# An encoder layer on one core: small loads awaited at the first transposes, the last query latents turned six units later, buffers from `hidden` on shifted by 32 bytes

## What is computed

```python
x = x + 0.5 * swiglu_ffn(rms_norm(x, ffn1_norm_g[l]), ffn1_w_gate[l], ffn1_w_up[l], ffn1_w_down[l])
h = rms_norm(x, mix_norm_g[l])
u = h @ w_in[l]
u_conv, c_q_raw, c_kv_raw, k_rope_raw, gl_conv, gl_mla = jnp.split(u, IN_SPLITS, axis=-1)
y_conv = conformer_conv_branch(u_conv, ...)      # 31-tap depthwise convolution, layer norm, silu, matmul
y_mla = mla_branch(c_q_raw, c_kv_raw, k_rope_raw, ...)   # 16 heads, q from 768 latents, k and v from 512
merged = jax.nn.sigmoid(gl_conv) * y_conv + jax.nn.sigmoid(gl_mla) * y_mla
x = x + merged @ w_out[l]
x = x + 0.5 * swiglu_ffn(rms_norm(x, ffn2_norm_g[l]), ffn2_w_gate[l], ffn2_w_up[l], ffn2_w_down[l])
return rms_norm(x, final_norm_g)
```

## Time and profile before

| | |
|---|---|
| median of 3 runs | 2376.14 us (2375.38 to 2376.43) |
| the profiled execution | 2375.09 us |
| its span, first to last instruction | 2373.1 us |
| mean granted TensorE clock | 0.996 |
| TensorE busy | 2319.3 us (98%), 10718 matmuls and transposes |
| VectorE, ScalarE busy | 1322.5 us (56%), 1188.6 us (50%) |
| DMA | 432.65 MB, 182 GB/s over the span |

### The profile page before, as it was taken

One profiled execution on the slowest core, in us unless ns is written; L12 is line 12 of the kernel. 1 busy time (PEld: TensorE's weight loads), 2 busy tenths in 40 slices (PEclk: granted clock), 3 DMA queues, 4 the chain that ended last, 5 costly groups with the idle time before them and its releaser, 6 DMA issues.

```text
span 2373.1 us, 26781 instructions
## 1 busy us (share of the span) xinstructions
PE 2319.3 (98%) x10718; PEld 1926.1 (81%) x10718; DVE 1322.5 (56%) x1469; ACT 1188.6 (50%) x1619; POOL 0.2 (0%) x4
## 2 busy tenths in 40 slices
PE   5999999999999999989999999999999999999997
PEld 4888888888888888868889878888888888888886
DVE  4554544544544588978876455655544544544443
ACT  5444444444444577777767564445444444444433
POOL 0000000000000000000000000000000000000000
PEclk9999999999999999999999999999999999999999
DMA  6666666666655655546643456556656656656663
GB/s 229 192 189 187 192 189 188 193 187 185 186 184 182 194 188 186 181 147 203 192 146 116 132 164 184 186 179 203 194 186 189 192 187 189 193 186 186 187 188 131
DMA packets 120588, 432.65 MB, mean 182 GB/s; under 512 B 13584, under 2 KB 13840, under 8 KB 120208
## 3 DMA queue, kind: packets, MB, share of 16 engines
q1 hardware_dynamic: 120464, 430.93, 58.7%
HBM read 428.78 MB, written 2.10 MB: 182 GB/s over the span
## 4 chain that ended last, share of the span: by engine, by line
PE 96%; DVE 2%; issue 1%; ACT 1%; DMA 1%; SPq 0%; ACTq 0%; DVEq 0%
PE bank L663 31%; PE bank L662 31%; PE bank L661 31%; PE turned L672 2%; PE bank L799 1%; PE bank L773 1%; PE bank L774 1%; DMA pos_i<-in_pos_in 0%; DVE q_rope L1083 0%; DVE w_lo L900 0%; ACT w_hi L422 0%; DVE q_rope L1089 0%; PE turned L784 0%; DMA raw<-in_ffn_up 0%; PE turned L853 0%
## 5 line engine op out<-in xcount | busy, mean ns | idle before, releaser
L900 DVE TENSOR_TENSOR w_lo<-raw,w_hi 128x1024 fp32r<-128x1024 f32 (+2 forms) x814 | 987.1, 1215 | 995.0 <-ACT w_hi L422 994.6
L422 ACT ACTIVATE w_hi<-raw 128x1024 fp32r<-128x1024 f32 (+2 forms) x814 | 853.6, 1052 | 1039.1 <-PE bank L663 1035.8
L661 PE MATMUL bank<-w_hi,h 128*128 128x512 f32 (+1 forms) x2144 | 836.3, 390 | 28.0 <-DMA pos_i<-in_pos_in 26.4
L663 PE MATMUL bank<-w_hi,h 128*128 128x512 f32 (+1 forms) x2144 | 833.4, 389 | 0.0
L662 PE MATMUL bank<-w_lo,h 128*128 128x512 f32 (+1 forms) x2144 | 833.2, 389 | 0.0
L661 PEld LDWEIGHTS bank<-w_hi,h 128*128 128x128 f32 x2144 | 403.7, 188 | 110.8 <-DMA pos_i<-in_pos_in 26.4
L663 PEld LDWEIGHTS bank<-w_hi,h 128*128 128x128 f32 x2144 | 403.3, 188 | 82.7
L662 PEld LDWEIGHTS bank<-w_lo,h 128*128 128x128 f32 x2144 | 403.5, 188 | 81.6
L661 PE MATMUL bank<-w_hi,hidden 128*128 128x512 f32 x704 | 278.8, 396 | 0.0
L662 PE MATMUL bank<-w_lo,hidden 128*128 128x512 f32 x704 | 278.4, 395 | 0.0
L663 PE MATMUL bank<-w_hi,hidden 128*128 128x512 f32 x704 | 278.4, 395 | 0.0
(11 more groups left out here) (167 smaller groups left out, 1223.2 us busy)
## 6 DMA issues: line engine op xcount, KB each, us to landing
raw<-in_ffn_up SPq DMA_DIRECT2D x352, 512.0 KB, 4.0
raw<-in_ffn_down SPq DMA_DIRECT2D x176, 512.0 KB, 3.6
raw<-in_conv_in SPq DMA_DIRECT2D x64, 512.0 KB, 3.9
raw<-in_conv_gate SPq DMA_DIRECT2D x32, 512.0 KB, 4.0
raw<-in_mla_gate SPq DMA_DIRECT2D x32, 512.0 KB, 4.2
raw<-in_mla_out SPq DMA_DIRECT2D x32, 512.0 KB, 3.6
raw<-in_conv_out SPq DMA_DIRECT2D x32, 512.0 KB, 3.7
raw<-in_w_out SPq DMA_DIRECT2D x32, 512.0 KB, 3.6
```

The source lines that it names most:

```text
L422: act.activation(w_hi[:, j, 0:n], raw[:, j, 0:n], ACT.Copy).then_inc(hi_ready, 1)
L661: pe.matmul(dst, fixed_hi, moving_hi, start=first, stop=False)
L663: return pe.matmul(dst, fixed_lo, moving_hi, start=False, stop=last)
L900: dve.tensor_tensor(w_lo[:, j, 0:n], raw[:, j, 0:n], w_hi[:, j, 0:n], ALU.subtract).then_inc(lo_ready, 1)
```

## The change

Six edits. TensorE's wait for the four small loads moves from ahead of unit 0 to the first turn (after unit 17). `x` is loaded in four column pieces, after units 4, 5, 6 and 7, instead of whole after unit 3; its squares, root and factor move one step later (7 and 8, and 9). ScalarE runs a copy of two zeros ahead of its first wait, with which its function table is loaded. The third turn of `cq_raw` and the turn of `k_rot` move from after unit 356 to after unit 362, and the work that takes them follows on ScalarE and VectorE at step 366. The turns back of the layer norm begin one unit later. And `before_hidden`, 8 floats a partition, stands ahead of `hidden`, so that `hidden` and all that is allocated after it (`attn`, `merged`, `c_kv`, `c_q` and the rest) begin 32 bytes later, at multiples of 64. `k_rot`'s turn now waits for 7 steps of `key_step` instead of 5.

```diff
--- before.py
+++ after.py
...
-TURNS = {"up": (2, 1, 1), "resid": (2, 2, 2), "glu": (2, 1, 0), "kv": (2, 2, 2), "q1": (3, 2, 2),
+TURNS = {"up": (2, 1, 1), "resid": (2, 2, 2), "glu": (2, 1, 0), "kv": (2, 2, 2), "q1": (2, 2, 2),
          "qrope": (2, 1, 0), "merge": (2, 1, 1)}
 
 TURN_AFTER = {"kv": 4, "q1": 5}
+
+LATE_TURN_AFTER = 11
...
+        self.q_turn = self.more_turns(1, 2, 2)
         self.k_turn = self.more_turns(1, 2, 0)
...
+        sb("before_hidden", [P, 8])
...
         hidden = sb("hidden", [P, FT, 2, T], F32R, outs)
...
-        FORE, BACK = M0 + 6, M0 + 20
+        FORE, BACK = M0 + 6, M0 + 21
...
             for u in range(KT // DEEP):
                 sp.dma_start(xt[:, DEEP * u:DEEP * (u + 1), :], xt_in[:, DEEP * u:DEEP * (u + 1), :]).then_inc(xt_loaded[u], 16)
                 load(u)
-                if u == 3:
-                    sp.dma_start(x[:, :, :], x_in).then_inc(x_loaded, 16)
+                if u >= 4:
+                    cols = slice(WIDE * (u - 4), WIDE * (u - 3))
+                    sp.dma_start(x[:, :, cols], x_in[:, :, cols]).then_inc(x_loaded, 16)
...
+            act.wait_ge(table_input, 1)
+            act.activation(root[:, :], total[:, :], ACT.Copy).then_inc(table_loaded, 1)
             act.wait_ge(gains_loaded, 16)
...
+                if u - AHEAD == Q_END + LATE_TURN_AFTER:
+                    take_late_turns()
-                if u == 8:
+                if u == 9:
                     take_root("x0")
-                if u in (6, 7):
-                    act.wait_ge(x_loaded, 16)
-                    tt = u - 6
+                if u in (7, 8):
+                    act.wait_ge(x_loaded, 64)
+                    tt = u - 7
...
             def turn_group(n):
                 g = groups[n]
+                if n == 1:
+                    pe.wait_ge(small_loaded, 64)
...
+            def late_turns():
+                pe.wait_ge(scaled, 4)
+                turn(plan.q_turn, cq_raw, 4 * P)
+                n = plan.k_turn
+                pe.wait_ge(*turn_freed(n - 2))
+                pe.wait_ge(key_step, 7)
+                for tt in range(2):
+                    last = pe.transpose(turned_bank[n % 2][:, tt * P:(tt + 1) * P],
+                                        k_rot[:, tt, :, :].rearrange("p d c -> p (d c)"), identity[:, :])
+                last.then_inc(turned, 1)
...
-            pe.wait_ge(small_loaded, 64)
             u = 0
...
                 turn_after(u)
+                if u == Q_END + LATE_TURN_AFTER:
+                    late_turns()
...
+            def take_late_turns():
+                dve.wait_ge(turn_hi, turns[plan.q_turn].hi_before + 2)
+                for r in range(2):
+                    dve.scalar_tensor_tensor(out=c_q[:, 4 + r, 1, :], in0=turned_bank[plan.q_turn % 2][:, r * T:(r + 1) * T],
+                                             scalar=gain["q"][:, 4 + r, :], in1=c_q[:, 4 + r, 0, :], op0=ALU.mult,
+                                             op1=ALU.subtract).then_inc(turn_lo, 1)
...
+            dve.memset(total[:, :], 0.0).then_inc(table_input, 1)
             dve.wait_ge(gains_loaded, 16)
...
                 if u == 8:
                     variance("x0", 1, D)
+                if u == 9:
                     factor("x0", rstd)
```

More of the change, by code:

```diff
@@ L293, in encoder @@
         scaled = sem("scaled")
+        table_input = sem("table_input")
+        table_loaded = sem("table_loaded")
         xt_hi = sem("xt_hi")
@@ L493, in take_turns @@
                         act.activation(q_rope[:, k:k + 2, 0, :], pair, ACT.Copy).then_inc(turn_hi, 1)
[L494 to L500, removed]
+            def take_late_turns():
+                act.wait_ge(turned, plan.q_turn + 1)
+                for r in range(2):
+                    act.activation(c_q[:, 4 + r, 0, :], turned_bank[plan.q_turn % 2][:, r * T:(r + 1) * T], ACT.Copy,
+                                   scale=gain["q"][:, 4 + r, :]).then_inc(turn_hi, 1)
+                t = turned_bank[plan.k_turn % 2]
+                act.wait_ge(turned, plan.k_turn + 1)
+                act.wait_ge(cleared, 4)
+                for j in range(2):
+                    rows = slice(ROPE * j, ROPE * (j + 1))
+                    act.activation(k_rope[rows, j, :], t[rows, 0:T], ACT.Copy).then_inc(turn_hi, 1)
             def make_tap(n):
@@ L733, in wait_stationary @@
                 elif g.stage == "q_rope":
-                    t = turns[plan.stage("latents")[2].turn + 2]
+                    t = turns[plan.q_turn]
                     pe.wait_ge(turn_lo, t.lo_before + t.lo)
@@ L950, in finish @@
                     if g.stage == "ffn1_down" and g.i == 0:
-                        dve.wait_ge(x_loaded, 16)
+                        dve.wait_ge(x_loaded, 64)
                     for tt in range(2):
```

## The result

| | before | after |
|---|---|---|
| median | 2375.76 us (2374.68 to 2376.43, 4 runs) | 2339.9 us (2339.5 to 2340.69, 4 runs) |
| profiled execution | 2375.09 us | 2340.69 us |
| its span | 2373.1 us | 2338.9 us |
| mean granted TensorE clock | 0.996 | 0.998 |

The ratio is 0.9851, 95% interval 0.9839 to 0.9864. The kernel became 35.9 us faster, where 49 were forecast: the direction was right, and the time lies 13.3 us above the forecast and 5.9 above the top of its range.

The account below looks back on a forecast made before the run. TensorE's stream was taken as the bound (96% of the span). Start 18.3, turn 10.0, layer norm 1.5 and addresses 19.7 sum to 49.5 us: 2325.6 from the profiled execution, 2326.6 as median; range 2321 to 2334.

Parts of the forecast that it names:

- The address term: Streams with `hidden`, `attn`, `merged`, `c_q` stationary: starting at multiples of 64 bytes gives `h`'s pace, 19.7 us (0 to 22).
- the shift does nothing: Rival on the buffers' addresses: moving them 32 bytes gains nothing, time 2346 us; chance 0.11.
- The start: Before unit 0: with the small-load wait moved, first matmul at 8.1 instead of 26.45 us; gain 18.3, at least 17.6.
- The table of the units' spare: Units 4 to 11 at the start: each ready before TensorE wants it, spare 4.1 down to 0.5 us; priced 0.
- The turn: Query latents' turn near unit 357: moving late transposes removes the 8.5 us wait and half clock; gain 10.0 (7.5 to 10.5).
- the 0.5 us of new waits: After the query latents' turn: VectorE, losing its pause, causes new short TensorE waits of 0.5 us, bounds 0 and 3.
- The layer norm: Layer norm's turns back: starting one unit later covers the 1.5 us wait; gain 1.5 us, 0 if the wait moves along.
- The rivals on the start: Start runs dry: slower `x` pieces or ScalarE detours make TensorE wait 2 to 6 us, 2329 to 2333; chance 0.08.
- on VectorE: Rival in the gate stages: VectorE's backlog makes TensorE wait in pieces, 2329 to 2333 us; chance 0.06.
- on slower: Rival after unit 357: continued waits drop the clock; above 2376 us if over 20 units run at half clock; chance 0.02.

## Why the prediction was wrong, point by point

**The address term failed, and it makes the miss.** It was put at 19.7 us and is 3.8 to 4.1 by the pad alone, and 4.9 in the table of places (1.4 + 1.7, and 1.8 in q_rope and the heads). By medians it was 15.9 too much, and the other three parts together gave 2.3 more than forecast; 49.5 - 15.9 + 2.3 = 35.9. The step that failed is "What differs is the byte at which they begin: 0 or 32 past a multiple of 64". The first half is true, and the runs show that the byte was the cause. The second half picked one property out of several in which 128 and 160 differ, and the trace of before had no buffer at a third multiple of 64 to tell them apart. `h` was fast because `w_hi` and `w_lo` begin at the same 128. The shift took `hidden` from 32 ahead of them to 64 ahead, 233 ns and 233 ns: **hidden 14.1 -> 0**. It took `attn` and `merged` from 96 behind to 64 behind, 233 to 229: **5.1 -> 3.1**. And it touched the heads, for which nothing was counted: **0 -> some 1.5**; `c_q` in q_rope gave 0.3 of its 0.5.

**The rival "the shift does nothing"** came nearer: 2346 against 2339.9. It would have been a better forecast for a wrong reason, since the address does count. What I should have had as a case of its own is a shift that misses, or helps only some of the buffers. The text had the bound, lower end 0, and then left it outside the range, with a chance of 0.11.

What the Trainium skill says (SBUF - State Buffer, Operand start alignment), that a start need only be a multiple of the element's size, is right for what runs; it gives no time, and the runs above differ by 13 us through starts alone. The lines of 16 bytes (same page, Specifications) don't tell these starts apart either: all are multiples of 32.

**The start was right in its mechanism and somewhat high in size.** 18.3 was forecast, at least 17.6. The first matmul came at 8.35 instead of 8.1, 18.1 earlier than before, of which 17.2 were left from unit 20 on; undone alone it was 18.7. The table of the units' spare held: no matmul waits between 8.35 and 994.83, and of units 4 to 11 the least spare is unit 11's, 1.3 us (0.5 said). Only the half pace at the beginning was not as assumed. I took the same 1.9 us before and after; it was 2.76, and those 0.8 are the gap between 18.1 and 17.2. How much of the start is owed to the early table load wasn't tried by itself.

**The turn was right.** 10.0 forecast, 10.5 between the two traces, 11.0 when undone. Unit 358 starts 11.1 us earlier (11.3 said), the six transposes cost 0.7 (0.8 said), and the 0.5 us of new waits didn't come: the wait of 0.41 ahead of unit 357 is the one that the text had already counted.

**The layer norm was right**: 1.5 forecast, and the wait of 1.5 is gone; when undone, 2.1 in its stage and 1.6 to 2.4 in the times.

**The rivals on the start, on VectorE and on slower** were wrong: no wait for data at the start, no row of waiting behind unit 357 beyond 0.41 us, granted clock 1.00 through the gate stages.

## What to carry to other kernels

When two streams of the same shape run at different paces with no wait in either, list every property in which their operands differ, pairs of operands too, and don't price a fix on the first that fits; a run that moves the *other* operand told here in one go what three moves of the first could not. For long streams of 512-column matmuls on the rounded form of float32, `fp32r` in the rows, as here, begin the stationary and the moving buffers at the same byte modulo 256 and look at the distance of starts in the trace. A wait that covers several loads should be split by who uses what.

## What the runs showed of the hardware that I had not expected

- The distance of the two operands' starts in SBUF, modulo 256 bytes, sets the pace of back-to-back 512-column matmuls (`fp32r` operands): 227 ns at 0, 229 at 64 behind, 232 at 128, 233 at 64 ahead, 233 to 234 at odd multiples of 32. At 256 columns, with `c_kv` stationary, it is 120 ns at 0, 117 to 118 at 64 behind and 114 to 115 at 64 ahead. Why isn't shown: the weight load of the next matmul runs beside the moving read of the present one, and a collision of the two reads would fit, but the mean weight load is 188 ns in the fast and in the slow streams alike, and no run separates the two.
- The time at half pace after the first matmul differs between traces of kernels with the same first instructions: full speed came 3.2 to 5.7 us after it (8.23 to 11.38 with `hidden` at 0, 8.35 to 14.06 in the changed kernel). Each kernel has one trace, so whether the kernel or the execution decides isn't shown. It is worth up to 1.2 us of a time, and is a reason not to read differences of 1 us between the times of single runs.
